# High parts first at the MLP entries and in the pooling unit, and four moved pieces of a two-block transformer kernel

## The chip, the cores and the metric

The kernel runs on one core of a Trainium2 chip. The metric is the device time of one launch in microseconds (us). Engines are named as the profile names them: PE is TensorE, PEld its weight loads, DVE is VectorE, ACT is ScalarE, POOL is GpSimd, SP is SyncE, which only issues DMAs here.

## The reference

Two transformer blocks over 1024 tokens of width 1024, in float32. What is computed, cut to its stages in their order:

```python
# block 1
u = rmsnorm(h, norm_mix);  proj = u @ w_in
attn = sliding_window_sink_attention(rope(aq), rope(ak), av, sinks)   # 8 heads, 2 kv heads, window 128
dn   = gated_deltanet(...)          # 4 heads of 128: conv, silu, chunked delta rule, norm, gate
h = h + concat(attn, dn) @ w_o
h = h + square(relu(rmsnorm(h, norm_mlp) @ w_up)) @ w_down            # width 4096
h = h + sigmoid(rmsnorm(h, norm_ple) @ w_ple_gate) * (p @ w_ple_proj)
x = rmsnorm(h, norm_final)
# block 2
u = rms_norm(x, norm_mix_2) @ w_in_2      # 256 pooling columns, then q, f, i, g of 768 columns
y = concat(pool_mixer(u_pool), hgrn2_mixer(q, f, i, g))               # 6 heads of 128
x = x + y @ w_out_2
x = x + square(relu(rms_norm(x, norm_mlp_2) @ w_up_2)) @ w_down_2
out = rms_norm(x, final_norm_2)
```

## The kernel before

The activations lie transposed: 8 tiles of 128 channels by 1024 tokens. A float32 product is made of three matmul passes over rounded parts, (w high, x high), (w high, x low) and (w low, x high), called passes 0, 1 and 2. A 128x1024 output of one weight tile needs two matmuls of 512 columns in each pass, so six matmuls for each of the 8 input tiles: 48 matmuls make a "unit" of one 128x1024 weight block, and its result is held in one of two pairs of PSUM banks (`pairs`); `mid` is the other half of PSUM.

Who makes the parts: the high part of x (`x_hi`) is a rounding copy by ACT (semaphore `hi_done`), the low part (`x_lo`) a subtraction by DVE (`x_ready`), which therefore comes after the high one. POOL rounds each unit's weights (`w_hi`, four pieces, L666) and subtracts (`w_lo`, four pieces, L670); it starts on a unit's weights when PE starts the unit before (`unit_started`). `part_of_product` (L721) issues matmuls for some input tiles and some passes.

Every engine runs its own queue in written order. The stages that the change touches, in time:

- Last delta head, `dn_head(3)`. Beside its small matmuls PE fills in the output projection w_o (`output_part`), whose input tile j needs x_hi and x_lo of the mixed activations. ACT makes x_hi tiles 0 to 5 in `dn_in` (L1458), three after each silu; DVE makes x_lo in `split_some` calls at L2053 to L2067.
- MLP (`mlp`, once in each block). Its entry is a unit (`proj_with_norm`, L820) that waits for x_ready of each tile, with the norm's sums between, and a second plain unit. Then come 217 steps of 12 matmuls, seven products of half size for each pair of blocks (a Strassen scheme): 105 up steps and 112 down steps. A step g writes to one of eight banks, `bank(g)` (L252). Step 4 waits until all four `first_y` readings of the two entry units are done (`up_y` 4). ACT rounds each step's weights (`part_hi`), POOL subtracts (L697, four pieces of 128 columns). In the first of four steps (m = 0) of each down product q of chunk c, PE waits for the low part (`h_lo`, DVE) of each of the four input pieces j. The inputs of the down steps come back from DRAM (`h_ops`).
- The gate of the per-layer input (8 units, `U_PLEG`), then the pooling unit `U_POOL` (L1217), whose input is the final h times a gain: x_hi by `gain12_hi` on ACT after the last gate unit, x_lo by `gain12_lo` on DVE. After this unit PE sums the squares of two norms (six sources).
- HGRN heads, `hg_head(h)`, six of them. In each, DVE multiplies the kept keys (`hkd`, L2705) after the third group of decays, and PE transposes them (L1307). In the last head PE fills in the output projection w_out_2 (`output_part`), units of 42 matmuls, each waiting at its first matmul for both weight parts (`w_split`).

Of the kernel before, what the change touches and what calls it, by code (L numbers as in the profile page):

```python
# [29 lines left out]
ACT = mybir.ActivationFunctionType  # L30
# [121 lines left out]
def build(nc, w_stream, w_up, w_down, x_t, p_t, params, pool_w, consts, att_masks, rope_cos, rope_sin, h_spill, h_ops,  # L152
          out_t):
    ctx = ExitStack()
    with ctx:
# [313 lines left out]
        for name in (  # L469
# [15 lines left out]
            "ple_in", "ple_hi", "ple_split", "ple_gate", "ple_mult",  # L485
# [227 lines left out]
        def _(pe):  # L713
# [7 lines left out]
            def part_of_product(unit, use, slot, pair, some, kts, col, stride, hi, lo, first=True, x_count=None,  # L721
                                passes=(0, 1, 2), enter=0, full=pair_full):


                for kt in some:
                    if kt == enter and first and 0 in passes:
                        pe.wait_ge(w_split, unit + 1)
# [6 lines left out]
                    for n in passes:  # L734
                        w, x = ((whi, hi), (whi, lo), (wlo, hi))[n]
                        for b in range(2):
                            ins = mm(pairs[:, pair, b * HALF:(b + 1) * HALF], w, x[kt][:, b * HALF:(b + 1) * HALF],
                                     kt == 0 and n == 0, kt == kts - 1 and n == 2)
                            if first and kt == enter and n == 0 and b == 0:
                                ins.then_inc(unit_started, 1)  # L740
                    if kt == kts - 1 and 2 in passes:
                        ins.then_inc(full, 1)
# [17 lines left out]
            def output_part(u0, v0, x_count, steps, passes=(0, 1, 2)):  # L760


                for step in steps:
                    for n in range(7 * step // 4, 7 * (step + 1) // 4):
# [3 lines left out]
                                        passes=passes)  # L768

# [50 lines left out]
            def proj_with_norm(unit, use, n, squares, x_count=None, full=pair_full):  # L820

                for kt in range(KT):
                    part_of_product(unit, use, unit % 2, use % 2, [kt], KT, 0, P, X_HI, X_LO, x_count=x_count, full=full)
                    if kt in (1, 3):
                        for j in range(2 * kt - 2, 2 * kt + 2):
                            square_sum(n, j, squares[j])
                    elif kt == KT - 3:
                        log_rows(n)


            def mlp(b, u0, v0, norm, split):
                def step(g, x, ready):
# [4 lines left out]
                    out = bank(g)  # L837
                    cols = [slice(j * P, (j + 1) * P) for j in range(4)]
                    for j in range(4):
                        if ready is not None:  # L840
                            pe.wait_ge(*ready(j))
                        mm(out, whi[:, cols[j]], hi[:, j, :], j == 0, False)
                        mm(out, whi[:, cols[j]], lo[:, j, :], False, False)
                    pe.wait_ge(s["part_lo"], b * STEPS + g + 1)
                    for j in range(4):
                        ins = mm(out, wlo[:, cols[j]], hi[:, j, :], False, j == 3)
# [4 lines left out]
                def bank_read(g):  # L851
# [4 lines left out]
                    elif g == 4:  # L856
                        pe.wait_ge(s["up_y"], b * NPAIR * 4 + 4)
# [1995 lines left out]
```

## Time and profile before

| | us |
|---|---|
| median of 3 runs | 2429.41 (2427.85 to 2430.82) |
| profiled execution, its own time | 2425.66 |
| span in its profile | 2423.8 |
| PE busy | 2360.0 (97%) |
| DVE busy | 1755.2 (72%) |
| POOL busy | 1688.9 (70%) |
| ACT busy | 949.2 (39%) |

The span runs from the first to the last instruction of the profiled execution. "Busy" is the union of an engine's instructions. A matmul of 512 columns is recorded with about 0.39 us, but the next one starts about 0.23 us after it, so consecutive ones overlap, and an idle time of PE in the profile begins only when the last one has drained. The granted clock of TensorE is given as a share of its full speed; over the whole span it is 0.995. Times in the text such as "at 597" are us from the start of this span.

### The profile page before, as it was taken

Reading aid. Unit: us, or ns where it says so; the run is one execution under the profiler, and the core shown is the slowest. Engines: PE = TensorE matmul, PEld = TensorE weight load, DVE = VectorE, ACT = ScalarE, POOL = GpSimd, SP = SyncE. Lnnn points to the kernel's source line nnn. Section 1 sums busy time; section 2 is a strip of 40 time slices with the busy share of each in tenths; the row PEclk is TensorE's granted clock in tenths of the full one; section 3 lists DMA queues with packets and bytes.
Section 4 is the critical chain, followed back from the end, with each engine's and each line's share of the span. In section 5 each row is a group of like instructions: output and inputs, shape, how many; then the busy total and the mean of one; then the engine's idle time right before and its main releaser. Section 6 shows DMA issues by size and latency. Waiting matters only on the chain.

```text
span 2423.8 us, 40271 instructions
## 1 busy us (share of the span) xinstructions
PE 2360.0 (97%) x15294; PEld 1884.6 (78%) x15294; DVE 1755.2 (72%) x2425; ACT 949.2 (39%) x1488; POOL 1688.9 (70%) x2442
## 2 busy tenths in 40 slices
PE   8999999999999999999999999999999999999997
PEld 5767777786888878888787788887778888888885
DVE  3685656639777787788755977778387777878877
ACT  3264223216433344444424344444163333344443
POOL 4623333547988888888676755666569888898885
PEclk9999999999999999999999999999999999999999
DMA  5200100211444465543022111112214444744342
GB/s 170 71 18 19 36 28 28 89 52 62 157 147 160 162 235 191 174 140 115 33 79 89 36 39 41 36 36 83 83 38 169 155 148 148 251 163 156 127 152 87
DMA packets 109719, 254.68 MB, mean 105 GB/s; under 512 B 9312, under 2 KB 9696, under 8 KB 107360
## 3 DMA queue, kind: packets, MB, share of 16 engines
q1 hardware_dynamic: 104112, 233.43, 28.3%
q10 hardware_dynamic: 5424, 18.75, 2.3%
q8 instruction: 122, 2.00, 0.3%
q14 instruction: 61, 0.50, 0.1%
HBM read 181.88 MB, written 67.63 MB: 103 GB/s over the span
## 4 chain that ended last, share of the span: by engine, by line
PE 82%; DVE 11%; POOL 3%; issue 2%; ACT 1%; DMA 1%; SPq 0%; DVEq 0%; ACTq 0%; POOLq 0%
PE pairs L715 52%; PE mid L715 29%; DVE res L1850 2%; DVE work_r L1850 2%; DVE work L1850 2%; POOL w_lo L697 2%; DVE work L2248 1%; DVE x_lo L1854 1%; DMA x_lo_raw<-h_ops 1%; DVE x_lo L1850 1%; PE mid L817 1%; POOL w_hi L666 1%; POOL w_lo L670 0%; DVE res L1945 0%; ACT work L1357 0%
## 5 line engine op out<-in xcount | busy, mean ns | idle before, releaser
L715 PE MATMUL pairs<-x_hi,w_hi 128*128 128x512 f32 x1576 | 540.0, 407 | 22.8 <-DVE work L2281 4.9
L715 PE MATMUL pairs<-x_lo,w_hi 128*128 128x512 f32 x1576 | 523.5, 396 | 0.0
L715 PE MATMUL pairs<-x_hi,w_lo 128*128 128x512 f32 x1576 | 476.1, 394 | 0.0
L697 POOL TENSOR_TENSOR w_lo<-w_raw,w_hi 128x128 fp32r<-128x128 f32 x600 | 386.9, 679 | 53.3 <-ACT w_hi L1357 53.3
L663 POOL TENSOR_TENSOR idle<-idle 128x1 f32<-128x1 f32 x77 | 20.2, 262 | 535.5 <-PE pairs L715 535.5
L715 PEld LDWEIGHTS pairs<-x_hi,w_hi 128*128 128x128 f32 x1576 | 281.1, 189 | 105.6 <-issue 28.6
L697 POOL TENSOR_TENSOR w_lo<-work,w_hi 128x128 fp32r<-128x128 f32 x512 | 312.5, 643 | 70.9 <-ACT w_hi L1357 68.8
L715 PEld LDWEIGHTS pairs<-x_hi,w_lo 128*128 128x128 f32 x1576 | 294.4, 189 | 62.3
L715 PEld LDWEIGHTS pairs<-x_lo,w_hi 128*128 128x128 f32 x1576 | 293.9, 189 | 62.1 <-issue 1.3
L670 POOL TENSOR_TENSOR w_lo<-w_raw,w_hi 128x256 fp32r<-128x256 f32 x308 | 308.9, 1033 | 6.4
L666 POOL TENSOR_SCALAR w_hi<-w_raw 128x256 fp32r<-128x256 f32 x308 | 301.9, 1005 | 0.0
L715 PE MATMUL pairs<-work_r,w_hi 128*128 128x512 f32 x1040 | 258.1, 390 | 0.0
L715 PE MATMUL mid<-work_r,w_hi 128*128 128x512 f32 x992 | 246.9, 390 | 4.7 <-DVE work_r L1850 4.4
L715 PEld LDWEIGHTS pairs<-work_r,w_hi 128*128 128x128 f32 x1040 | 195.0, 188 | 41.8 <-issue 1.2
L715 PEld LDWEIGHTS mid<-work_r,w_hi 128*128 128x128 f32 x992 | 185.8, 188 | 45.6 <-DVE work_r L1850 7.2
L1850 DVE TENSOR_TENSOR work<-work 128x512 f32<-128x512 f32 (+4 forms) x190 | 176.3, 941 | 34.3 <-DMA work<-res 21.5
L1357 ACT ACTIVATE w_hi<-work 128x512 fp32r<-128x512 f32 x128 | 80.6, 631 | 240.1 <-DVE work L1850 94.6
L1357 ACT ACTIVATE w_hi<-w_raw 128x512 fp32r<-128x512 f32 (+1 forms) x152 | 96.4, 636 | 197.3 <-PE pairs L715 70.7
L697 POOL TENSOR_TENSOR w_lo<-x_lo_raw,w_hi 128x128 fp32r<-128x128 f32 x256 | 148.5, 615 | 11.7 <-ACT w_hi L1357 11.7
L697 POOL TENSOR_TENSOR w_lo<-w_sum,w_hi 128x128 fp32r<-128x128 f32 x240 | 133.5, 585 | 22.6 <-ACT w_hi L1357 22.6
L715 PE MATMUL mid<-x_hi,w_hi 128*128 128x512 f32 x376 | 146.4, 389 | 0.0
L715 PE MATMUL mid<-x_lo,w_hi 128*128 128x512 f32 x376 | 146.4, 389 | 0.0
(223 smaller groups left out, 3930.8 us busy)
## 6 DMA issues: line engine op xcount, KB each, us to landing
h_ops<-work SPq DMA_DIRECT2D x224, 256.0 KB, 3.9
w_raw<-w_stream SPq DMA_DIRECT2D x80, 512.0 KB, 3.5
w_raw<-w_up SPq DMA_DIRECT2D x120, 256.0 KB, 3.3
out_sq<-h_ops SPq DMA_DIRECT2D x28, 1024.0 KB, 5.2
x_lo_raw<-h_ops SPq DMA_DIRECT2D x28, 1024.0 KB, 5.4
work<-w_down SPq DMA_DIRECT2D x16, 1024.0 KB, 5.0
out_sq<-w_down SPq DMA_DIRECT2D x8, 1024.0 KB, 6.0
x_lo_raw<-w_down SPq DMA_DIRECT2D x8, 1024.0 KB, 5.5
```

The costliest lines, as they stand in the source:

```text
L663: nc.gpsimd.tensor_tensor(idle[:, 0:1], idle[:, 1:2], idle[:, 1:2], ALU.add)
L666: ins = nc.gpsimd.tensor_scalar(w_hi[:, slot, part], w_raw[:, slot, part], 1.0, None, ALU.mult)
L670: ins = nc.gpsimd.tensor_tensor(w_lo[:, slot, part], w_raw[:, slot, part], w_hi[:, slot, part], ALU.subtract)
L697: ins = nc.gpsimd.tensor_tensor(low[:, part], raw[:, part], high[:, part], ALU.subtract)
L715: return nc.tensor.matmul(out, w, x, start=start, stop=stop)
L817: ins = nc.tensor.transpose(dst[:, c * P:(c + 1) * P], src[:, c * P:(c + 1) * P], ident)
L1357: return nc.scalar.activation(out, in_, func, **kw).then_inc(sem_out, 1)
L1850: return nc.vector.tensor_tensor(out, a, b, op).then_inc(sem_out, 1)
L1854: nc.vector.scalar_tensor_tensor(x_lo[:, j, :], res[:, j, :], par[:, gain + j:gain + j + 1], x_hi[:, j, :], ALU.mult, ALU.subtract).then_i ...
L2248: nc.vector.scalar_tensor_tensor(out, src, g, less, ALU.mult, ALU.subtract).then_inc(s["t_sum"], 1)
```

## The change

It does this:

1. MLP entry units and the pooling unit: PE goes over the tiles with passes 0 and 2 as soon as x_hi of the tile is there, and does pass 1 of a tile three tiles later, when x_lo is there. 48 matmuls as before.
2. `bank(g)` takes the pair of the MLP's first unit into account, and steps 4, 5 and 6 wait for 2, 3 and 4 readings (`up_y`) in place of 4 at step 4.
3. Two down steps of each MLP, (c, q, m) = (0, 0, 0) and (3, 6, 0), do the pass over x_lo last.
4. The norm sums after the pooling unit move into it, ahead of pass 1 of tiles 6 and 7. ACT makes x_hi of tiles 0 to 6 during the last gate unit, each when PE has used the tile (`ple_x_used`), and DVE's x_lo of tiles 0 to 2 moves ahead.
5. Last HGRN head: a unit of w_out_2 starts when its high weights are there, and its first low-weight pass comes seventh of 21.
6. Last delta head: ACT's x_hi 3, 4, 5 move behind the output square and the norm's exponentials; DVE's splits move one place forward.
7. Kept keys are multiplied before the third group of decays in the first and in the last HGRN head.

```diff
-        def bank(g):
+        def bank(g, v0):
-            return mid[:, g % 8, :] if g % 8 < 4 else pairs[:, g % 8 // 2 - 2, (g % 2) * HALF:(g % 2 + 1) * HALF]
+            return mid[:, g % 8, :] if g % 8 < 4 else pairs[:, (g % 8 // 2 + v0) % 2, (g % 2) * HALF:(g % 2 + 1) * HALF]
...
                 for kt in some:
                     if kt == enter and first and 0 in passes:
+                        if early:
+                            pe.wait_ge(w_hi_done, unit)
+                        else:
+                            pe.wait_ge(w_split, unit + 1)
+                    if early and kt == enter and 2 in passes:
                         pe.wait_ge(w_split, unit + 1)
...
+            LATE_LOW = (((0, 0), (0, 1), (1, 0)), ((1, 1), (2, 0), (2, 1)), ((0, 2), (3, 0), (3, 1)),
+                        ((1, 2), (4, 0), (4, 1)), ((2, 2), (5, 0), (5, 1)), ((3, 2), (6, 0), (6, 1)),
+                        ((4, 2), (5, 2), (6, 2)))
+            def output_late_low(u0, v0, x_count, step):
+                for n in range(7 * step // 4, 7 * (step + 1) // 4):
+                    m, place_ = divmod(n, KT - 1)
+                    for kt, p in LATE_LOW[place_]:
+                        part_of_product(u0 + m, v0 + m, (u0 + m) % 2, (v0 + m) % 2, [kt], KT - 1 if m < KT - 1 else KT,
+                                        0, P, X_HI, X_LO, x_count=x_count if m == 0 and p == 0 else None, passes=(p,),
+                                        early=True)
...
+            X_LAG = 3
+            def high_first(unit, use, t, x_count, full=pair_full):
+                if t < KT:
+                    pe.wait_ge(hi_done, x_count + t)
+                    part_of_product(unit, use, unit % 2, use % 2, [t], KT, 0, P, X_HI, X_LO, passes=(0, 2), full=full, final=1)
+                if t >= X_LAG:
+                    pe.wait_ge(x_ready, x_count + t - X_LAG)
+                    part_of_product(unit, use, unit % 2, use % 2, [t - X_LAG], KT, 0, P, X_HI, X_LO, passes=(1,), full=full,
+                                    final=1)
...
-                    elif g == 4:
-                        pe.wait_ge(s["up_y"], b * NPAIR * 4 + 4)
+                    elif g in (4, 5, 6):
+                        pe.wait_ge(s["up_y"], b * NPAIR * 4 + g - 2)
...
+                            lo_last = m == 0 and (c, q) in ((0, 0), (DCH - 1, 6))
...
-            proj(U_POOL, V_POOL, U_POOL, V_POOL, x_count=4 * KT + 1)
-            pe.wait_ge(acc_done, 5 * KT - 4)
-            pe.wait_ge(sq_done, 5 * KT)
...
+            for t in range(KT + POOL_LAG):
+                if t < KT:
+                    pe.wait_ge(hi_done, 4 * KT + t + 1)
+                    part_of_product(U_POOL, V_POOL, U_POOL % 2, V_POOL % 2, [t], KT, 0, P, X_HI, X_LO, passes=(0, 2),
+                                    final=1)
+                if t >= POOL_LAG:
+                    pe.wait_ge(x_ready, 4 * KT + 1 + t - POOL_LAG)
+                    part_of_product(U_POOL, V_POOL, U_POOL % 2, V_POOL % 2, [t - POOL_LAG], KT, 0, P, X_HI, X_LO, passes=(1,),
+                                    final=1)
+                if t == KT:
+                    pe.wait_ge(acc_done, 5 * KT - 4)
+                    pe.wait_ge(sq_done, 5 * KT)
...
                 for n in range(2):
                     dn_silu(h, n)
-                    if h == DN_H - 1:
-                        dn_mix_hi(*range(3 * n, 3 * n + 3))
+                    if h == DN_H - 1 and n == 0:
+                        dn_mix_hi(0, 1, 2)
...
                     dn_square(h - 1)
+                    if last:
+                        dn_mix_hi(3)
                     dn_out_norm(h - 1)
...
+                    dn_mix_hi(4, 5)
                     act.wait_ge(s["o_step"], 1 + bump(h, 2, 0))
...
                 if m == KT - 1:
-                    act.wait_ge(pair_full, V_POOL)
-                    gain12_hi([0])
+                    for j in range(KT - 1):
+                        act.wait_ge(res_done, j + 1)
+                        act.wait_ge(s["ple_x_used"], j + 1)
+                        gain12_hi([j])
...
-                    split_some(1, 2)
+                    split_some(1, 2, 3)
                     dn_normed(h - 1)
-                    split_some(3, 4)
+                    split_some(4)
...
-                    split_some(5)
+                    split_some(5, 6)
...
+                def kept_keys():
+                    dve.wait_ge(s["h_exp"], bump(h, 3, 3))
+                    tt(B[4][:, 0:KEPT], B[4][:, 0:KEPT], A[5][:, 0:KEPT], ALU.mult, s["hkd"])
                 if last:
+                    kept_keys()
                     hg_take(h, 3)
                 decays(2)
                 merge(0, 1)
+                if 0 < h and not last:
+                    kept_keys()
```

## Rows read from the trace of the kernel before

**Rows 1.** The page: busy time of the engines, and one costly group of matmuls.
```profile
PE 2360.0 (97%) x15294; PEld 1884.6 (78%) x15294; DVE 1755.2 (72%) x2425; ACT 949.2 (39%) x1488; POOL 1688.9 (70%) x2442
...
L715 PE MATMUL mid<-work_r,w_hi 128*128 128x512 f32 x992 | 246.9, 390 | 4.7 <-DVE work_r L1850 4.4
```
**Rows 2.** Waits of PE, whole span: total us, times, longest us.
```profile
PE pairs L715 <- DVE work L2281: 4.9, 2, 2.5
PE mid L715 <- DVE work_r L1850: 4.4, 4, 1.2
PE pairs L715 <- DVE x_lo L1854: 3.7, 4, 1.2
PE pairs L715 <- DVE x_lo L2494: 3.1, 2, 2.7
...
PE mid L817 <- DVE work L1850: 2.6, 1, 2.6
...
PE pairs L715 <- POOL w_lo L670: 2.4, 2, 2.2
```
**Rows 3.** Chain of waits, in time: start, us, what. Near the end of the first MLP.
```profile
1168.69 10.88 PE pairs L715 x48
```
**Rows 4.** Windows, PE: length, busy (instructions), granted clock, DMA share, GB/s.
```profile
1299.70:1303.50 3.80, 3.76 (x10) 0.56 0.00 0
...
597.40:601.00 3.60, 3.57 (x16) 1.00 0.29 111
```
**Rows 5.** Timeline, last delta head: start, us, instruction, [idle before, releaser].
```profile
422.31 2.94 ACT L1357 ACTIVATE x_hi<-work 128x1024 fp32r<-128x1024 f32 x3
...
427.64 0.64 PE L715 MATMUL mid<-tmp,cst 128*32 128x256 f32 x8 [1.58 <-ACT tmp L1357]
...
435.64 0.73 PE L715 MATMUL pairs<-x_hi,w_hi 128*128 128x512 f32 x2 [0.49 <-DVE x_lo L1850]
...
444.40 0.74 PE L715 MATMUL pairs<-x_hi,w_hi 128*128 128x512 f32 x2 [2.27 <-DVE x_lo L1850]
```
**Rows 6.** Timeline of DVE, PE and POOL, steps 0 to 12 after the MLP entries.
```profile
587.77 1.28 DVE L2281 SCALAR_TENSOR_TENSOR work<-pairs,r_tok 128x512 f32<-128x512 f32 x2
...
596.09 1.29 DVE L2281 SCALAR_TENSOR_TENSOR work<-pairs,r_tok 128x512 f32<-128x512 f32 x2
...
597.43 0.50 PE L715 MATMUL pairs<-x_hi,w_hi 128*128 128x512 f32 x1 [2.47 <-DVE work L2281]
...
606.91 9.14 POOL L697 TENSOR_TENSOR w_lo<-w_raw,w_hi 128x128 fp32r<-128x128 f32 x12 [2.34 <-ACT w_hi L1357]
...
1828.51 9.14 POOL L697 TENSOR_TENSOR w_lo<-w_raw,w_hi 128x128 fp32r<-128x128 f32 x12 [2.35 <-ACT w_hi L1357]
```
**Rows 7.** Chain of waits, first down steps of the first MLP.
```profile
861.61 0.33 SPq L539
...
864.74 10.80 DMA x_lo_raw<-h_ops
...
897.19 2.94 POOL w_lo L697 x4
```
**Rows 8.** Timeline of PE, the stops at the first down step and near the last.
```profile
874.74 0.74 PE L715 MATMUL mid<-work_r,w_hi 128*128 128x512 f32 x2 [0.93 <-DVE work_r L1850]
...
1160.71 1.59 PE L715 MATMUL mid<-work_r,w_hi 128*128 128x512 f32 x4 [1.23 <-DVE work_r L1850]
```
**Rows 9.** Timeline around the pooling unit.
```profile
1290.55 5.19 POOL L670 TENSOR_TENSOR w_lo<-w_raw,w_hi 128x256 fp32r<-128x256 f32 x4
...
1303.18 9.11 DVE L2494 SCALAR_TENSOR_TENSOR x_lo<-res,stat,x_hi 128x1024 fp32r<-128x1024 f32 x6
...
1306.72 6.17 POOL L670 TENSOR_TENSOR w_lo<-w_raw,w_hi 128x256 fp32r<-128x256 f32 x4
```
**Rows 10.** Timeline, first and last HGRN head, DVE and POOL.
```profile
1386.05 2.42 DVE L1850 TENSOR_TENSOR work<-work,res 128x896 f32<-128x896 f32 x2
...
1680.26 4.95 POOL L670 TENSOR_TENSOR w_lo<-w_raw,w_hi 128x256 fp32r<-128x256 f32 x4
```

More of the change, by code:

```diff
@@ L818, in transposes, with proj_with_norm, step @@
                 ins.then_inc(sem_out, 1)
[L820 to L825, printed above, removed]
+            X_LAG = 3
[7 more added lines that the diff above has]
+                                    final=1)
+            def proj_with_norm(unit, use, n, squares, x_count, full=pair_full):
+                for t in range(KT + X_LAG):
+                    high_first(unit, use, t, x_count, full)
+                    if t in (1, 4):
+                        for j in range(0 if t == 1 else 4, 4 if t == 1 else KT):
                             square_sum(n, j, squares[j])
-                    elif kt == KT - 3:
+                    elif t == KT - 1:
                         log_rows(n)
             def mlp(b, u0, v0, norm, split):
-                def step(g, x, ready):
+                def step(g, x, hi_ready, lo_ready, lo_last=False):
                     pe.wait_ge(s["part_hi"], b * STEPS + g + 1)
@@ L836, in step @@
                     hi, lo = x
-                    out = bank(g)
+                    out = bank(g, v0)
                     cols = [slice(j * P, (j + 1) * P) for j in range(4)]
[L839 to L846, printed above, removed]
+                    if not lo_last:
+                        for j in range(4):
+                            if lo_ready is not None:
+                                pe.wait_ge(*lo_ready(j))
+                            mm(out, whi[:, cols[j]], hi[:, j, :], j == 0, False)
+                            mm(out, whi[:, cols[j]], lo[:, j, :], False, False)
+                        pe.wait_ge(s["part_lo"], b * STEPS + g + 1)
+                        for j in range(4):
+                            ins = mm(out, wlo[:, cols[j]], hi[:, j, :], False, j == 3)
+                    else:
+                        for j in range(4):
+                            pe.wait_ge(*hi_ready(j))
+                            mm(out, whi[:, cols[j]], hi[:, j, :], j == 0, False)
+                        pe.wait_ge(s["part_lo"], b * STEPS + g + 1)
+                        for j in range(4):
+                            mm(out, wlo[:, cols[j]], hi[:, j, :], False, False)
+                        for j in range(4):
+                            pe.wait_ge(*lo_ready(j))
+                            ins = mm(out, whi[:, cols[j]], lo[:, j, :], False, j == 3)
                     ins.then_inc(s["step_done"], 1)
@@ L1629, in mlp @@
                             act.wait_ge(s["up_h"], (b * NPAIR + i) * 4 - 2)
-                        a(quad[0], bank(g), ACT.Copy, s["snap"])
+                        a(quad[0], bank(g, v0), ACT.Copy, s["snap"])
                     for ahead in {0: (), U_STEPS + 2: (), U_STEPS + 3: (3, 4), U_STEPS + 5: (), U_STEPS + 6: (3, 4)}.get(g, (4,)):
@@ L2328, in up_step @@
                     elif k == 4:
-                        tt(quad[0], quad[0], bank(g + 4), ALU.add, s["up_step"])
+                        tt(quad[0], quad[0], bank(g + 4, v0), ALU.add, s["up_step"])
                         dve.wait_ge(s["up_step"], n + 5)
@@ L2334, in up_step @@
                     elif k == 5:
-                        tt(quad[2], quad[2], bank(g + 5), ALU.add, s["up_step"])
+                        tt(quad[2], quad[2], bank(g + 5, v0), ALU.add, s["up_step"])
                         dve.wait_ge(s["up_step"], n + 6)
@@ L2342, in up_step @@
                     elif k == 6:
-                        tt(quad[1], quad[1], bank(g + 6), ALU.add, s["up_step"])
+                        tt(quad[1], quad[1], bank(g + 6, v0), ALU.add, s["up_step"])
                         dve.wait_ge(s["up_step"], n + 7)
@@ L2380, in add @@
                     def add(out, sem_out):
-                        tt(out, out, bank(g), ALU.add, sem_out)
+                        tt(out, out, bank(g, v0), ALU.add, sem_out)
                     g, last = step_index(c, q, m), c == DCH - 1
@@ L2512, in _ @@
                     two_adds(m - 1)
-            gain12_lo(range(2, KT))
+            gain12_lo(range(3, KT))
             dve.wait_ge(s["two_act"], 2)
```

73 lines of the change are left out of this document (41 added, 32 removed).

## The prediction

> **What bounds the kernel now.** I read the page first [rows 1]: PE is busy 97% of the span and the next engine 72%, so time can only come from PE's work or from its stops. The work stays the same here: each unit keeps 48 matmuls, each step 12. A stretch without waits shows their price, 48 matmuls in 10.88 us, 0.227 us each [rows 3]. So the whole question is stops. The list of PE's waits [rows 2] names those this change is about: first_y readings 4.9 us, h_lo 4.4, the entry splits 3.7, the pooling splits 3.1, the kept keys 2.6, a unit's low weights 2.4. A matmul is recorded with 0.39 us [rows 1] and the next could start after 0.227, so each stop costs its idle time and 0.16.
>
> Then the granted clock [rows 4]: after the stop before the pooling unit the next 3.8 us ran at 0.56 of full speed, that is mostly at 1.2 GHz, and cost 3.8 x 0.44 = 1.7 us more. There are four such windows in the trace, at 1300, 1388, 1685 and 1819, each behind a stop of 2.2 to 2.7 us; the stop of 2.47 us at 597 had none (clock 1.00 behind it). The Trainium skill (TensorE: Matmul & The Clock Gate, Part 1) says that activity releases a throttle and that where a slow stretch falls varies from run to run; the first agrees with these rows, the second one trace can't show.
>
> The last view is the chain of waits, which tells whether a stop on PE is on the path at all. That decides two parts below.
>
> **Part by part.**
>
> *Last delta head.* Stops of 1.58, 0.49 and 2.27 us [rows 5], with 3 x 0.16: 4.8 us. At 427.6 PE waits for a square that ACT does behind three x_hi copies (2.94 us); with these moved it is there 2.9 us earlier, more than the 1.74 at stake. The other two stops wait for x_lo of tiles 3 and 6. Tile 3 is now split before dn_normed; tile 6, which stood behind two small subtractions that wait for PE's sums and ACT's exponential, comes before them. What is late next: x_hi 4 and 5, now behind the norm's exponentials, 0.98 us each, then x_lo 6. Laying DVE's queue out at 1.5 us a split beside POOL (9.11/6, [rows 9]), x_lo 6 is ready about 0.6 us ahead of PE. I take 4.8, from 2.9 (the last stop stays half) to 5.0.
>
> *Entry of each MLP.* The four stops of both entries have 3.7 us idle [rows 2], 2.2 per MLP with the overruns; high-first needs only x_hi, which ACT has long made, and the bank pair, free when the next to last residual is added. So PE comes 2.05 us earlier to step 4, due at 597.43 - 2.63 = 594.80 [rows 6], now 592.75. Step 4 needs only the second reading, done at 589.05. Step 5 starts at 595.5 but needs the third reading, which DVE ends at 596.75 (596.09 and half of 1.29): DVE's chain of splits does not move, so a stop of 1.3 us is new there. Step 5 starts 596.8 instead of 600.15, ahead by 3.35. Then POOL: its low weights for steps 9 to 11 end at 616.05 (606.91 + 9.14), tied through ACT to DVE. PE needs 0.91 us for the last four matmuls, so step 12 can't start before 616.95; it was at 597.43 + 8 x 2.72 = 619.2. I take 2.3 for the first MLP (bounds 1.3 and 3.4). In the second MLP the same row of POOL ends at 1837.65, so step 12 at 1838.6; before it was 1818.7 + 1.8 (half clock) + 21.8 = 1842.3. I take 4.0 (bounds 2.3 and 5.3).
>
> *First down step, low x last.* The stop of 0.93 us at 874.74 [rows 8], with overrun 1.1, twice. It goes, but the chain does not pass there [rows 7]: it goes from SP's weight load behind an up step (861.61) over the read of h_ops (864.74, 10.8 us), then ACT and DVE, to POOL's low weights at 897.19, for which PE stands a moment at 900. None of these is moved by PE being earlier at 874, so PE waits 1.1 us more at 900. I take 0, from 0 to 1.1 in each MLP. The entry's gain survives here, since 861.61 hangs on PE's own steps.
>
> *Step (3, 6, 0), low x last.* The stop stands at 1160.71 [rows 8]. The stretch of 48 matmuls without a wait from 1168.69 [rows 3] ends at 1179.57, one step before the MLP's end at 1182.3. Counted back from there in steps of 2.72 us, 1160.5 is the start of the eighth from the end, which is (3, 5, 0). The edit names (3, 6, 0), the fourth from the end, which starts about 1171.4, inside the stretch without a wait. So this stop stays: 0 (it would be 1.4 each).
>
> *Pooling unit.* 3.1 us of idle, two overruns 0.3, half clock 1.7: 5.1, and some small stops of 0.1 to 0.2 between tiles. ACT makes x_hi 0 to 6 in the last gate unit, about 1 us each (2.94/3, [rows 5]; these seven and the sigmoid fit in its idle time there). x_hi 7 hangs on take, sigmoid, product and sum, some 6 us behind the last gate matmul; PE has 36 matmuls, 8.2 us, before it. x_lo 3 to 7 then leave DVE about every 1.5 us [rows 9]; PE wants x_lo 5 about 0.4 us before it is there, and the norm sums stand between it and tile 6. They need ACT's last squares, ready about when PE gets there. The norm sums cost the same inside. I take 5.2 (bounds 2 and 5.8): the rest of that stage is driven from PE and shifts along.
>
> The danger is POOL. Its low weights of the pooling unit end at 1295.74 (1290.55 + 5.19), and DVE's new splits, laid out behind the last sums, now run until about 1296.8, an estimate. With DVE splitting all the time the same four pieces took 6.17 us [rows 9], which gives 1296.7, and PE wants them at 1296.9, where the unit's first matmul now stands without its stop (1299.7 less 2.7 and the overrun). The Trainium skill (SBUF — State Buffer, Who interferes with whom) says that a DVE operation with two inputs in SBUF and a POOL operation that reads SBUF exclude each other. The rows agree in direction, 1.54 us a piece against 1.30; if each excluded the other for its whole length the sum would be 1 us smaller.
>
> *First HGRN head, kept keys.* Idle 2.6 and overrun 0.16 [rows 2], half clock 1.6: 4.3. DVE's product (half of the 2.42 at 1386.05, [rows 10]) now comes before the queries, about 5 us earlier. ACT's third exponentials come 1.1 us later for it, and PE, 4.3 earlier at the next score products, waits about 0.9 for DVE. I take 3.4 (bounds 1.6 and 4.3).
>
> *Last HGRN head.* POOL's low weights end at 1685.21 (1680.26 + 4.95, [rows 10]); PE stood 2.4 us in two stops [rows 2], 2.7 with overruns, and lost 1.7 at half clock. With high weights first PE starts at 1682.9 (1685.3 less 2.2 and the overrun) and needs the low ones after 12 matmuls, 2.7 us on, at 1685.65. The kept keys are wanted some 1.4 us behind the start; as DVE's queue lies in the old order they would come about 3.3 us too late, in the new one, ahead of the third decays, about 3.8 us early (estimates). So these two edits only pay together. I take 4.2 (bounds 2.5 and 4.5).
>
> Sum: 4.8 + 2.3 + 4.0 + 0 + 0 + 5.2 + 3.4 + 4.2 = 23.9 us. The profiled execution took 2425.66 (span 2423.8 and 1.9 around it), so its like would take 2401.8. The median of the runs, 2429.41, is 3.75 above that execution; I keep the distance: 2405.5 us.
>
> **Rivals.**
>
> *Given back in the MLPs.* DVE, POOL and the read of h_ops could hold back what the entries gain: 6.3 us lost, 2411.8. For it: POOL and DVE are the next to stop PE behind the entry [rows 6], and 861.61 to 900 is a chain without PE [rows 7]. Against it: that chain starts from PE's step.
>
> *Half clock stays.* Shorter stops remain at 597, 1160, 1381 and others; if the slow windows come there instead, 6.6 us of the sum don't come: 2412.1. For it: windows came behind some stops of 2.3 us and not behind others [rows 4]. Against it: none came behind a stop under 2 us.
>
> *More than forecast.* The down entry pays (2.2) and POOL does not cap the entries (2.3): 2401.0. For it: POOL's cap rests on 0.3 us per step. Against it: rows 7.
>
> *Slower.* The entries and the pooling unit now wait twice per tile. If such a unit ran wholly at 1.2 GHz, each of its 48 matmuls would cost about 0.2 us more (the 1.7 us of a window are eight of them, [rows 4]), 9.6 us a unit. With all three units that is 28.8 lost on the forecast: 2434. With two it is 2425, still faster; it decides from 23.9/9.6, two and a half units. Against it: PE's stops of 0.4 to 1.2 us at the entries now leave the clock at full.
>
> **How the numbers follow.** Forecast 0.53; given back 0.16; half clock stays 0.15; more 0.12; slower 0.04. The range, 2398 to 2417, holds the first four with 1.5 us of spread below and 5 above, where two losses may meet. A measurement of this kernel tells 0.2% (4.9 us) from no change. Every case but the last is more than 10 us faster, 0.96 together; I take 0.02 of that for losses that add up to no change, and of the last case's 0.04 a quarter for the units between two and three: faster 0.94, same 0.03, slower 0.03.
>
> **What would show it.** In the profile after: no PE stop over 0.5 us between 425 and 446; at the MLP entry one stop of 1 to 1.5 us before step 5, released by first_y, and short ones for L697 in steps 9 to 11; at the third down product longer stops for L697 (about 1.4 us); a stop of about 1.2 us for h_lo still there, seven steps before each MLP's end; the norm sums at about 11 us after the last gate matmul; no clock of 0.5 before the final stage. A PE stop before the pooling unit released by POOL, or a half clock in a high-first unit, would make it wrong.

## The result, and the profile after

| | before | after |
|---|---|---|
| median of 4 runs | 2428.63 us (2423.97 to 2430.82) | 2406.18 us (2404.49 to 2407.61) |
| profiled execution, span | 2423.8 us | 2405.8 us (its own time 2407.61) |
| PE busy | 2360.0 us | 2354.3 us |

The ratio of after to before is 0.9906, 95% interval 0.9892 to 0.9921. Forecast were 2405.5 us and a gain of 23.9; measured are 2406.2 and 22.4 between the medians. The two profiled executions lie only 18.05 us apart (2425.66 and 2407.61): the forecast for such an execution was 2401.8, so it came out 5.8 us too long. The terms have to be held against the traces one by one.

The page of the kernel after, busy time of the engines:

```profile
PE 2354.3 (98%) x15294; PEld 1881.2 (78%) x15294; DVE 1756.4 (73%) x2425; ACT 947.8 (39%) x1488; POOL 1687.1 (70%) x2442
```

The number of instructions is that of before on each engine [rows 1]. PE's waits over the whole span, kernel after (total us, times, longest us):

```profile
PE mid L715 <- POOL w_lo L697: 3.4, 6, 0.8
PE mid L715 <- DVE res L1916: 2.8, 2, 1.9
...
PE mid L715 <- DVE work_r L1916: 2.5, 2, 1.2
PE pairs L715 <- DVE work L1916: 2.5, 3, 1.2
...
PE pairs L715 <- DVE work L2346: 1.9, 2, 0.9
...
PE pairs L715 <- DVE x_lo L2559: 0.9, 1, 0.9
```

Against [rows 2], the entry splits and the kept keys are gone from the list. The first_y readings (L2346 now) fell from 4.9 to 1.9 us, the pooling splits from 3.1 to 0.9, h_lo from 4.4 to 2.5. Three things have grown: the wait for POOL's low weights of a step (L697, 0.3 us before), `res` by DVE (0.9 before; the added stop is for the operands of the third score products), and `work` by DVE at `pairs` (1.2 before; the added stop is for the bank of a unit in the last head). The stops themselves, timeline of PE in the kernel after (start, us, instruction, [idle before, releaser]):

```profile
592.97 0.50 PE L715 MATMUL pairs<-x_hi,w_hi 128*128 128x512 f32 x1 [0.93 <-DVE work L2346]
...
606.15 1.21 PE L715 MATMUL mid<-work_r,w_lo 128*128 128x512 f32 x4 [0.18 <-POOL w_lo L697]
...
609.65 1.20 PE L715 MATMUL mid<-work_r,w_lo 128*128 128x512 f32 x4 [0.45 <-POOL w_lo L697]
...
894.15 1.19 PE L715 MATMUL mid<-work_r,w_lo 128*128 128x512 f32 x4 [0.85 <-POOL w_lo L697]
...
1154.65 1.60 PE L715 MATMUL mid<-work_r,w_hi 128*128 128x512 f32 x4 [1.23 <-DVE work_r L1916]
...
1301.88 0.73 PE L715 MATMUL pairs<-x_lo,w_hi 128*128 128x512 f32 x2 [0.95 <-DVE x_lo L2559]
...
1684.69 0.70 PE L715 MATMUL pairs<-x_hi,w_hi 128*128 128x512 f32 x2 [1.23 <-DVE work L1916]
```

Between 425 and 446 there is no stop left. The second MLP has the same three stops behind its entry (0.95, 0.57 and 0.49 us idle). The last view is the granted clock, windows of the kernel after (length, PE busy and instructions, clock, DMA share, GB/s), at the pooling unit, the first and the last HGRN head, and the second MLP's entry:

```profile
1300.00:1303.40 3.40, 2.43 (x21) 1.00 0.00 0
1383.00:1386.40 3.40, 3.40 (x31) 0.50 0.45 154
1684.70:1688.00 3.30, 3.30 (x15) 1.00 1.02 413
1803.60:1807.00 3.40, 3.39 (x15) 1.00 0.48 178
```

Of the four slow stretches of before [rows 4] one is left, and it stands behind the new stop for the operands. (At the very end, where PE has no matmul left to do, every trace shows 0.50 for 13 to 16 us; it costs nothing and is left out here and below.)

PE issues the same number of matmuls in every kernel here, so stages can be cut at the same matmul (the 3700th, 4100th and so on that PE starts) and their lengths compared. In us, worked out from the matmul starts in each trace; "again" is a second profiled execution of the same kernel (below), and "s" marks a slow stretch inside. The stages that are not listed differ by 0.1 us or less:

```
stage                     forecast   before  again     after   again     gain of the two pairs
start to last delta head      0      390.46  392.85    392.03  393.30s   -1.6, -0.5
last delta head              4.8      66.46   69.60s    61.12   61.16     5.3,  8.4
first MLP's entry            2.3      85.41   87.01s    83.21   83.25     2.2,  3.8
steps around first down       0       58.91   58.97     58.81   58.88     0.1,  0.1
end of the first MLP          0      127.56  127.55    127.58  127.55     0.0,  0.0
pooling unit                 5.2      45.72s  45.77s    41.31   41.26     4.4,  4.5
first HGRN head              3.4      35.75s  34.18     34.92s  33.37     0.8,  0.8
last HGRN head               4.2      91.13s  90.31     88.20   87.90     2.9,  2.4
second MLP's entry           4.0      86.94s  85.50     83.61   83.59     3.3,  1.9
its first down steps          0       70.53   70.47     70.21   70.22     0.3,  0.3
all                         23.9                                         18.0, 21.8
```

### The profile page after: what moved, and what is told of

The parts are those of the page before. It is cut to its first block, busy times and chain, and to the rows that moved or that the text cites. A ratio compares the mean times of both kernels' runs of the same rounds, so it can differ in the third digit from the quotient of the medians.

```text
span 2405.8 us, 40281 instructions
## 1 busy us (share of the span) xinstructions
PE 2354.3 (98%) x15294; PEld 1881.2 (78%) x15294; DVE 1756.4 (73%) x2425; ACT 947.8 (39%) x1488; POOL 1687.1 (70%) x2442
## 4 chain that ended last, share of the span: by engine, by line
PE 79%; DVE 13%; POOL 2%; issue 2%; ACT 1%; DMA 1%; SPq 0%; DVEq 0%; ACTq 0%; POOLq 0%
PE pairs L715 50%; PE mid L715 28%; DVE res L1916 3%; POOL w_lo L697 2%; DVE work L1916 2%; DVE work_r L1916 2%; DVE x_lo L1920 1%; DVE work L2313 1%; DVE x_lo L1916 1%; DVE tmp L1916 1%; PE mid L835 0%; DMA x_lo_raw<-h_ops 0%; ACT work L1418 0%; DVE res L2011 0%; DVE x_lo L2559 0%
## 5 line engine op out<-in xcount | busy, mean ns | idle before, releaser
L697 POOL TENSOR_TENSOR w_lo<-w_raw,w_hi 128x128 fp32r<-128x128 f32 x600 | 386.7, 678 | 57.0 <-ACT w_hi L1418 57.0
L697 POOL TENSOR_TENSOR w_lo<-work,w_hi 128x128 fp32r<-128x128 f32 x512 | 312.7, 644 | 70.9 <-ACT w_hi L1418 68.8
L697 POOL TENSOR_TENSOR w_lo<-x_lo_raw,w_hi 128x128 fp32r<-128x128 f32 x256 | 148.0, 613 | 11.5 <-ACT w_hi L1418 11.5
L697 POOL TENSOR_TENSOR w_lo<-w_sum,w_hi 128x128 fp32r<-128x128 f32 x240 | 132.8, 582 | 17.4 <-ACT w_hi L1418 17.4
```

The lines of the kernel that those rows point to most:

```text
L697: ins = nc.gpsimd.tensor_tensor(low[:, part], raw[:, part], high[:, part], ALU.subtract)
```

## The experiments

**Controls: both kernels once more.**

> The kernel before once more, to see how far two executions of one kernel differ. The profiled executions are 18.05 us apart (2425.66 and 2407.61), the medians 22.5. Theory A (chance of the execution): the same stops as in the first profile within 0.1 us each, another number or place of the windows at half clock, time 2424 to 2431. Theory B (the first profile is typical and the medians are not): 2425 to 2426 again, four windows in the same places.

Measured: 2428.81 us (10 runs), ratio to the same kernel's other runs 0.9995 (0.9985 to 1.0004). The stops came back within 0.2 us, with one more: 0.58 us idle at the last head's transposes, 2.2 us behind the stop at 1690.83. In the first execution the slow stretch at 1685 lies just there; PE comes to the transposes later by it, and the stop is not there. Of the four slow stretches only the one at the pooling unit came back (here at 1307.5). Windows of PE in this second execution, the last three where the first one was slow:

```profile
447.40:454.20 6.80, 6.80 (x28) 0.50 1.00 401
604.40:607.80 3.40, 3.40 (x10) 0.50 0.25 59
1307.50:1310.90 3.40, 3.40 (x9) 0.50 0.00 0
1388.00:1391.00 3.00, 3.00 (x74) 1.00 0.00 0
1685.00:1688.00 3.00, 3.00 (x15) 1.00 0.00 0
1818.00:1821.00 3.00, 3.00 (x14) 1.00 0.57 178
```

Theory A holds. The sum of the slow time was the same by luck, 13.65 us in both.

> The changed kernel once more. Theory A: the stops of the first profile return within 0.1 us (1.10 and 1.12 at step 5 of the MLPs, 2.07 in the first HGRN head, 1.43 in the last), the window at half clock behind 1382 may be missing, 2404 to 2408. Theory B (the window belongs to the stop of 2.07 us): it is there again, 3.4 us long, behind the same stop. Ratio to the kernel before 0.990 to 0.992.

Measured: 2408.19 us (2407.04 to 2409.03, 5 runs), ratio 0.9915 (0.9901 to 0.9928). The stop for the operands came back, without its slow stretch, the row and the window behind it:

```profile
1383.52 1.51 PE L715 MATMUL mid<-res,work 128*32 128x96 f32 x48 [1.93 <-DVE res L1916]
```
```profile
1383.50:1386.90 3.40, 3.38 (x56) 1.00 0.54 154
```

So theory A again. Whether the clock falls behind this stop differs between executions of one kernel, the stop itself does not. One part alone is worth 0.5 to 6 us and the intervals of the ratios are about 3.5 us either way, so for single parts the stage lengths decide, and the medians stand beside them.

**The entry: which half of it works.** One kernel takes the order of passes back and keeps the rest:

```diff
-                for t in range(KT + X_LAG):
-                    high_first(unit, use, t, x_count, full)
...
+                for kt in range(KT):
+                    part_of_product(unit, use, unit % 2, use % 2, [kt], KT, 0, P, X_HI, X_LO, x_count=x_count, full=full)
...
```

> The changed kernel, but the first unit of each MLP goes over its tiles as before (three passes of a tile, then the next); the bank pair and the later waits for first_y stay. Theory 1 (DVE's readings and POOL's low weights set step 12, as forecast): the stops of 1.38 and 0.77 us return, but the stop of 1.10 at step 5 and those of 0.35 and 0.61 (0.73 and 0.65) for POOL go, so each MLP loses 0 to 0.4 us and the kernel 0 to 1. Rival (high-first pays by itself): 2.15 us per MLP, 4.3 in all.

Measured: 2407.28 us, 0.9913 (0.9898 to 0.9928). The two stops at the entry are back, and the ones behind it are all but gone (timeline of PE in this kernel, all stops between 550 and 612):

```profile
553.32 0.70 PE L715 MATMUL pairs<-x_hi,w_hi 128*128 128x512 f32 x2 [1.21 <-DVE x_lo L1919]
...
555.55 0.73 PE L715 MATMUL pairs<-x_hi,w_hi 128*128 128x512 f32 x2 [0.61 <-DVE x_lo L1919]
...
610.73 1.20 PE L715 MATMUL mid<-work_r,w_lo 128*128 128x512 f32 x4 [0.41 <-POOL w_lo L697]
```

The entry's stage takes 83.35 us against 83.23, the second MLP's 83.83 against 83.60. High-first at the entry is worth 0.1 to 0.2 us per MLP. The other kernel keeps it and waits for all readings at once:

```diff
-                    elif g in (4, 5, 6):
-                        pe.wait_ge(s["up_y"], b * NPAIR * 4 + g - 2)
+                    elif g == 4:
+                        pe.wait_ge(s["up_y"], b * NPAIR * 4 + 4)
```

> The changed kernel, but step 4 waits for all four first_y readings, as before the change; high-first stays. Theory 1: the fourth reading comes where it came before (597.43 less the 3.6 us that all lies earlier), so PE stops 4.8 us before step 4 in place of 1.1 + 0.35 + 0.61 later: 2.8 us per MLP, and 0 to 1.8 for half clock behind it, 5.6 to 9 us in all; high-first alone brings nothing. Rival (high-first brings its 2.15 us per MLP by itself): a loss of 0.3 to 1 per MLP, 0.6 to 2 in all.

Measured: 2417.34 us, 0.9952 (0.9936 to 0.9967); stages of 87.32 and 87.66 us, 4.1 more in each MLP. The stop and the clock around it and its like in the second MLP:

```profile
594.57 0.80 PE L715 MATMUL pairs<-x_hi,w_hi 128*128 128x512 f32 x1 [4.40 <-DVE work L2346]
```
```profile
592.30:599.10 6.80, 4.54 (x11) 0.50 0.55 156
1807.40:1814.20 6.80, 5.25 (x12) 0.50 0.59 199
```

Theory 1 in both: DVE's readings set the time, and what PE gains ahead of them is a longer stop. Nearly the whole gain of the entry is the three waits of one reading each. From 594.57 to the end of the slow stretch at 599.05 PE lost 2.2 us (half of 4.48), so without the clock this stage would take 85.1 us; before the change it took 85.4 without a slow stretch. In the second MLP PE lost 2.6 us (half of 5.25), which leaves 85.0 against 85.5. High-first alone is worth 0.3 to 0.5.

**The last delta head undone.**

```diff
-                    split_some(1, 2, 3)
+                    split_some(1, 2)
                     dn_normed(h - 1)
-                    split_some(4)
+                    split_some(3, 4)
...
-                    split_some(5, 6)
+                    split_some(5)
...
+                split_some(6)
```

and x_hi 3 to 5 back behind the second silu.

> The changed kernel with the last delta head as before (x_hi 3 to 5 and the splits in their old places). Theory 1 (the three stops were the whole of it): 1.74, 0.65 and 2.43 us return at about 428, 436 and 444, 4.8 us, and a window at half clock may follow (1.7 or 3.4 us more), 2411 to 2417. Rival (the stop moves on to the next wait, so that part was given back): under 3 us.

Measured: 2414.25 us, 0.9940 (0.9924 to 0.9956). The three stops are back to the hundredth:

```profile
429.43 0.64 PE L715 MATMUL mid<-tmp,cst 128*32 128x256 f32 x8 [1.57 <-ACT tmp L1418]
...
437.43 0.73 PE L715 MATMUL pairs<-x_hi,w_hi 128*128 128x512 f32 x2 [0.49 <-DVE x_lo L1913]
...
446.17 0.73 PE L715 MATMUL pairs<-x_hi,w_hi 128*128 128x512 f32 x2 [2.27 <-DVE x_lo L1913]
```

The stage takes 69.55 us with a slow stretch of 6.8 us, against 61.15: 8.4 us. Before the change it took 66.46 without a slow stretch, so 5.3 of them are the stops and 3.1 the clock. All stages behind it keep their lengths. Theory 1.

**The pooling unit in the old order.** The loop over t is `proj(...)` again, with the norm sums behind it; the earlier copies and splits stay.

> The changed kernel, but PE goes over the tiles of the pooling unit with all three passes and sums the norms behind it, as before; the earlier copies and splits stay. Theory 1: x_lo 3 is ready at 1298.3, where this order wants it at 1295.4, so a stop of 2.9 us and some of 0.2; the unit ends at 1305.6, the sums (1.5 us) at 1307.1 in place of 1305.2: 1.9 us lost, 3.6 with a window at half clock. Rival (the earlier copies carry the gain and the order nothing): under 0.5 us.

Measured: 2410.21 us, 0.9927 (0.9910 to 0.9943); the stage takes 44.30 us against 41.26, 3.0 more, with no slow stretch in it. The stops:

```profile
1293.80 0.73 PE L715 MATMUL pairs<-x_hi,w_hi 128*128 128x512 f32 x2 [0.37 <-DVE x_lo L2550]
...
1298.14 0.74 PE L715 MATMUL pairs<-x_hi,w_hi 128*128 128x512 f32 x2 [2.68 <-DVE x_lo L2550]
```

Theory 1 in kind, 1.1 us too small in size. Before the change the stage took 45.7 with a slow stretch of 1.7, that is 44.0 without. So the earlier copies by themselves bring nothing; the order, with the copies in place, brings the 3.0, and some 1.5 is the clock. What the order would bring without the earlier copies was not run.

**Kept keys of the first HGRN head undone** (the product stands behind the third decays again).

> The changed kernel with the kept keys of the first HGRN head behind the third decays again. Theory 1 (the third score products wait for DVE's operands whatever comes before): the stop of 2.7 us before the transposes returns and the one of 2.1 us before the score products goes, 0.4 to 0.9 us lost and nothing more. Theory 2 (the term as forecast, less the clock: the edit brings 1.8 us, 3.4 with a window): 1.8 us or more lost.

Measured: 2409.71 us, 0.9922 (0.9905 to 0.9939); the stage takes 35.70 us with a slow stretch, and the changed kernel's takes 34.92 with one: 0.8 us. The stop is back at the transposes, and no stop follows at the score products:

```profile
1376.67 1.76 PE L835 MATMUL mid<-cst,work 128*128 128x128 f32 x7 [2.60 <-DVE work L1916]
```

Theory 1.

**The last HGRN head, one edit at a time.** First the late low weights without the early kept keys, then the early kept keys with units that wait for both weight parts (`output_part` in place of `output_late_low`).

> The changed kernel, but the kept keys of the last HGRN head come behind the third decays again; the late low weights stay. Theory 1 (the two edits only pay together, as forecast): the transposes are wanted 1.6 us behind the unit's start and the kept keys end about 1676.9 on the first profile's time in place of 1669.3, a stop of 4.0 us; the stop of 1.1 to 1.4 us for the bank goes, net 2.6 to 2.9 us lost, 4.3 to 4.6 with a window at half clock. Rival (each edit carries half): 1.4 us lost.

> The changed kernel with w_out_2 in the old order of passes, so that a unit waits for both weight parts at its start; the kept keys stay early. Theory 1: the first unit stands 2.3 us for POOL's low weights and the stop for the bank goes, net 1.0 to 1.3 us lost, 2.7 to 3.0 with a window at half clock, and nothing at the transposes. Rival (each edit carries half): 1.4 us without a stop for the weights' low part alone.

Measured: 2410.15 us, 0.9922 (0.9905 to 0.9938), stage 93.14 us; and 2408.42 us, 0.9917 (0.9901 to 0.9934), stage 89.39 us. Both edits: 87.90 and 88.20. Before: 90.31 and 91.13. The stop of each kernel, and the clock behind the first:

```profile
1674.47 1.76 PE L835 MATMUL mid<-cst,work 128*128 128x128 f32 x7 [3.27 <-DVE work L1916]
```
```profile
1673.40:1680.20 6.80, 5.73 (x17) 0.50 0.62 196
```
```profile
1672.77 0.74 PE L715 MATMUL pairs<-x_hi,w_hi 128*128 128x512 f32 x2 [1.98 <-POOL w_lo L670]
```

The order alone made the head 2 to 3 us slower than before. Counted at the same matmuls against the second execution of the changed kernel, PE is 3.43 us behind after the stop and 6.18 at the end of the slow stretch, so the clock cost 2.7; without it the head would take 90.4, as long as before. The kept keys alone bring 0.9 (90.31 to 89.39), the two together 2.4. Against both edits, the order alone loses 5.2 us (2.5 without the clock), the kept keys alone 1.5. Both of theory 1's stops are there, 3.4 us where it had 4.0 and 2.1 where it had 2.3. The edits do pay more together than their sum, but "only pay together" was too strong.

**The low part last, one product earlier, and two more moves.**

```diff
-                            lo_last = m == 0 and (c, q) in ((0, 0), (DCH - 1, 6))
+                            lo_last = m == 0 and (c, q) == (DCH - 1, 5)
```

> The changed kernel, but the step that does its pass over x_lo last is (3, 5, 0) alone, in place of (0, 0, 0) and (3, 6, 0). Theory 1 (the stop was one product earlier than the edit, and the first down step is given back): the stops of 1.39 and 0.3 us before the MLPs' ends go, 3.3 us gained in all; at the first down step 1.1 us return and the 0.99 us for POOL's low weights twenty microseconds later become 0.33, net 0. 2404 to 2405.5. Rival (the high part is as late as the low one, or the first down step pays): 0 or a loss of up to 2.2 us.

Measured: 2403.91 us (2403.49 to 2407.02, 5 runs), 0.9902 (0.9888 to 0.9916). The ends of the MLPs (in the second one up to the end of the kernel) take 126.42 and 259.87 us against 127.55 and 260.95: 1.1 us each, not 1.65. The new order reads the first low part by the ninth matmul of the step in place of the second, but the fourth by the twelfth in place of the eighth, only 0.9 us later. DVE makes the third and fourth in the first row here and ends them at 1155.37, and PE stands for the fourth until 1155.42 (second row). At the first down step the stop is back and POOL's behind it is short again (next rows), and the stages around it keep their length (58.92 and 70.23 us):

```profile
1153.56 1.81 DVE L1916 TENSOR_TENSOR work_r<-out_sq,work_r 128x512 fp32r<-128x512 f32 x2
...
1155.42 2.33 PE L715 MATMUL mid<-work_r,w_hi 128*128 128x512 f32 x9 [0.37 <-DVE work_r L1916]
```
```profile
868.65 0.73 PE L715 MATMUL mid<-work_r,w_hi 128*128 128x512 f32 x2 [0.87 <-DVE work_r L1916]
...
894.14 1.21 PE L715 MATMUL mid<-work_r,w_lo 128*128 128x512 f32 x4 [0.25 <-POOL w_lo L697]
```

Both halves of theory 1 hold, the first with two thirds of its size. The last kernel adds two moves to it:

```diff
                 if h == 0:
                     ...
-                    queries()
...
                 merge(1, 0)
+                if h == 0:
+                    queries()
...
+                if last:
+                    residual(0)
                 operands(2)
...
-                if last:
-                    residual(0)
...
                 mix_hi_used(5, 6)
+                if last:
+                    for j in range(KT - 1):
+                        act.wait_ge(x_ready, 5 * KT + j + 1)
+                        act.dma_start(mix[:, j, :], h_spill[:, j, :]).then_inc(x_in[j], 16)
                 exps(2)
...
-                    for j in range(KT - 1):
-                        act.wait_ge(x_ready, 5 * KT + j + 1)
-                        act.dma_start(mix[:, j, :], h_spill[:, j, :]).then_inc(x_in[j], 16)
```

> The changed kernel with three more moves: the step that does x_lo last is (3, 5, 0) alone; in the first HGRN head DVE's queries come behind the second merge; in the last head the loads of the residual are issued before the third exponentials and the first residual is scaled before the third operands. Theory: the first gives 2.3 to 2.6 us (1.1 to 1.3 per MLP, as its own run's profile shows); the second takes 1.2 us from the chain to the operands, so the stop of 2.1 becomes 0.9; the third lets the bank's reading start up to 1 us earlier, so the stop of 1.1 becomes 0.2 to 0.7. Sum 4.1 to 4.8 us: 2402 to 2403. Rival (each of these stops moves on to the wait behind it: the second merge's readers, the state products, the third operands): only the first gain is left, 2404 to 2406.

Measured: 2402.68 us, 0.9890 (0.9874 to 0.9907). The first head fell to 31.91 us (from 33.37), the stop for the operands to 0.49 us idle. But the last head took 89.52 us, with two new stops for POOL's low weights, behind one strange row. One of its four pieces, at 1645.71, took 9.48 us. Timeline of PE and then of POOL in this kernel:

```profile
1663.36 0.73 PE L715 MATMUL pairs<-x_hi,w_lo 128*128 128x512 f32 x2 [1.33 <-POOL w_lo L670]
...
1674.57 0.74 PE L715 MATMUL pairs<-x_hi,w_lo 128*128 128x512 f32 x2 [0.61 <-POOL w_lo L670]
```
```profile
1644.08 12.98 POOL L666 TENSOR_SCALAR w_hi<-w_raw 128x256 fp32r<-128x256 f32 x4
```

Is POOL late because PE is early, or by chance?

> The same kernel as the last one, once more. In its first profile one rounding of 128x256 on POOL took 9.48 us at 1645.7 (the same one took 1.43 in the other kernels), PE then stood 1.49 and 0.77 us for the low weights behind it, and that execution was 2.2 to 2.6 us above the three timed ones. Theory 1 (chance of that execution): the instruction takes 1.4 us again, both stops are gone, span about 2400.7, median 2402 to 2403. Theory 2 (POOL is late because the second move lets PE come earlier): the 9.48 us and the stops come back, and the median of the timed runs stays below the profiled one only by chance.

Measured: 2401.47 us (2399.99 to 2403.07, 5 runs), 0.9891 (0.9874 to 0.9909). The same four pieces, and the last head at 86.96 us, with neither stop:

```profile
1644.46 4.14 POOL L666 TENSOR_SCALAR w_hi<-w_raw 128x256 fp32r<-128x256 f32 x4
```

The piece took 1.43 us this time: chance, theory 1. The move in the first head brings 1.45 us there and the two in the last head together 0.95, the kernel with all three is some 5 us faster than the changed one (2407.5, the median of its nine runs) and 26 us faster than before.

## Why the prediction was right, and where not

The total held: 22.4 us measured between medians, 23.9 forecast; slow stretches included, the traces give 18.0 and 21.8. Its way over the profiled execution did not hold: that one was forecast at 2401.8 and took 2407.6, and the median, put 3.75 us above it, lies 1.4 below it. That these two misses meet at 2406.2 is luck. The gain between medians does not hang on them; by the nine runs of the changed kernel and the ten more of the one before (2407.5 and 2428.8) it is 21.3. Six points by its own steps:

- *Last delta head*, 4.8: right. 5.3 without a change of clock. x_lo 6 is ready ahead of PE, as forecast, and by 1.2 us in place of about 0.6 (DVE ends it at 439.55, PE reads it from 440.78).
- *Entries*, 2.3 and 4.0: right in size (2.2; 1.9 without and 3.3 with the clock's part) and in the places of the new stops: 1.10 before step 5 (forecast 1.3), then POOL's at 606 and 610. The two readings of the chain were the right ones: DVE's third reading and POOL's pieces for steps 9 to 11. What the prediction did not say, though it follows from its numbers, is that high-first itself is then worth nothing. It was listed as 2.2 us of gain and taken back by two caps; the run without it shows 0.1 to 0.2. A slip in the working: the numbers for the second MLP give 1842.3 less 1838.6, that is 3.7, where the sum has 4.0.
- *First down step* 0 and *step (3, 6, 0)* 0: right, both shown. For the first, the chain after goes as before from SP over the read of h_ops, now 10.76 us, to POOL's pieces at 891.17 (rows below). The stop for these pieces is 1.0 us with its overrun (0.85 idle), where 1.4 was forecast. The second was a matter of counting steps back from the end; moving the edit by one product gives 1.1 us per MLP.

```profile
858.76 10.76 DMA x_lo_raw<-h_ops
...
891.17 2.94 POOL w_lo L697 x4
```

- *Pooling unit*, 5.2: measured 4.45. The term that was off is x_lo 5, "0.4 us before it is there": 1.1 us. DVE needed 1.60 us a split beside POOL (last fence of this list, 7.98/5), not 1.5, and the four of them that lie beside POOL's subtractions start 1.68 us apart. The danger named there was near: POOL's low weights of this unit end at 1290.70, and PE starts the unit at 1290.82.
- *Kept keys in the first head*, 3.4: this term failed, as did the sign "no clock of 0.5 before the final stage"; measured is 0.8. The edit's place was right and the stop of 2.7 went. The new wait was put at "about 0.9 for DVE". PE came 4.3 us earlier to the score products and DVE's operands 0.9 later against the rest, so 0.9 would need 4.3 us of slack before. The trace of before shows the operands ready at 1391.89 (1388.39 + 3.50) and PE there at 1395.18, 3.3 us (rows below). That leaves 1.9, and the stop measured is 1.91 idle. It is also long enough for the clock to fall behind it, which it did in 3 of 9 executions with this stop. Kernel before:

```profile
1388.39 3.50 DVE L1850 TENSOR_TENSOR res<-res,work 128x768 f32<-128x768 f32 x3
...
1395.18 1.51 PE L715 MATMUL mid<-res,work 128*32 128x96 f32 x48
```

- *Last head*, 4.2: measured 2.9 and 2.4. The two edits did what was said, but the next unit needs its bank, which DVE empties only after its residual product: nothing in the prediction took up that wait. Rows of DVE in the pooling unit and before both new stops, kernel after:

```profile
1296.71 7.98 DVE L2559 SCALAR_TENSOR_TENSOR x_lo<-res,stat,x_hi 128x1024 fp32r<-128x1024 f32 x5
...
1378.76 3.49 DVE L1916 TENSOR_TENSOR res<-res,work 128x768 f32<-128x768 f32 x3
...
1682.01 1.28 DVE L2669 SCALAR_TENSOR_TENSOR work<-work,par,res 128x1024 f32<-128x1024 f32 x1 [0.34 <-DMA work<-h_spill]
1683.32 1.22 DVE L1916 TENSOR_TENSOR work<-work,pairs 128x1024 f32<-128x1024 f32 x1
```

The operands end at 1382.25 and PE starts at 1382.30; the bank is empty at 1684.54 and PE starts at 1684.69.

How could the total hold? Take the four slow stretches out of both sides. The forecast has 17.1 us of stops in its 23.9 (the rest is 1.7, 1.6, 1.7 and 1.8 for the clock at 1300, 1388, 1685 and 1819); measured in stages without a slow stretch are 5.3 + 2.2 + 2.8 + 0.8 + 2.4 + 1.9 = 15.4 (the 2.8 of the pooling unit is its 4.5 less 1.7, as both executions of before were slow there). The stops were forecast 1.7 us too high. In the second pair the clock gave the other 6.8 of the stages' 22.2, as forecast in sum, but not in place: it stood in the delta head, at the first MLP's entry and at the pooling unit, so the first two gained 8.4 and 3.8 and the heads less. In the first pair it gave only 4.0 of 19.4. One stretch was left in the first head. The one at 1685, priced at 1.7, was worth 0.8 (91.13 against 90.31), since the other execution has the stop of 0.58 there that the slow stretch took the place of; the one at 1819 was worth 1.4. That the sum of the slow time was the same in both traces of before is luck. The second pair (2428.85 and 2407.04) lies near both medians and shows 21.8; the first one had an execution of before that was 3 us short. The stretch up to the last delta head is 0.5 to 1.6 us longer in the changed kernel's traces. It differs by 2.4 us between the two executions of before (390.5 and 392.9) and takes 391.8 to 393.7 in the twelve traces that have the change or most of it, so the short one is the exception; whether the change has a part in it stays open.

Of the rivals, *half clock stays* happened in part: one stretch in the first profile. *Given back in the MLPs* did not go beyond the two caps in the forecast, *more than forecast* failed at the first down step, and no unit ran at half clock because of its double waits.

## What to carry to other kernels

- When a stop goes, write down for every wait behind it how long its releaser had been done before PE came, from the rows. The gain ends at the smallest of these slacks: here 3.3 us at the operands and the bank in the last head. Include the waits for a free bank, not only those for data.
- If a later wait is tied to an engine whose queue the change does not move, work ahead of it is worth nothing, and splitting that one wait into one per reading is worth nearly all of it (1.4 to 2.1 us per MLP here and 4.1 with the clock, against 0.1 to 0.5).
- Compare two traces by stages cut at the same matmul, and take two executions of each: that separates a stop, which here returned within 0.2 us (the bank's within 0.33), from the clock, which mostly did not. A slow stretch is not always worth half its length either: a short stop behind it can go by it.

## What the runs showed of the hardware

- Whether the clock falls behind a stop of PE differs between executions of the same kernel, and longer stops had it more often. Counted from 400 us on over twelve traces, all but the two of the last kernel (a stop is its idle time and 0.16): the three of 3.4 to 4.6 us all had a slow stretch, 6.8 us long; of fifteen of 2.3 to 2.9 us nine had one; of ten of 2.0 to 2.15 three; of three of 1.73 to 1.74 and the many of 0.5 to 1.5 none. Outside this count, two traces have a stretch at 307, 1.2 us behind a stop of 1.7 us among small matmuls, so a stop under 2 us had one too. A stretch lasted 3.4 or 6.8 us at 0.50, 1.2 GHz. Between two executions of one kernel one of 3.4 us made its stage 1.4 to 1.6 us longer, once only 0.8. In the 4.4 us stop it had begun 2.3 us before PE went on. The Trainium skill (TensorE: Matmul & The Clock Gate, Part 1) says that activity releases the throttle, and that the point of transition varies from run to run. The traces agree: the counted stretches stand behind stops of PE, and they moved between executions.
- One rounding of 128x256 on POOL took 9.48 us instead of 1.43 in one of two executions of one kernel, with nothing else changed, and cost PE 2.3 us in two stops 18 and 29 us later. A profile is one execution; a stop that stands behind such a row is not the kernel's.
- A split of 128x1024 by DVE and a subtraction of 128x256 by POOL, each with two inputs, slow each other down. Side by side around 1300 in the kernel after they keep one pace, 1.68 us each; alone DVE's takes 1.27 (at 1303.42) and POOL's 0.73 (at 1688.78).
